# Second FFN's down projection and the per-layer embedding by blocks of 512 tokens, with bf16 copies of their weights in DRAM

## What is computed

```
h = x
h = h + 0.5 * rms(swiglu(rms(h), W_gate, W_up, W_down))        # FFN1, d_ff = 5632
h = h + rms(token_mixing(rms(h)))                              # 8 FoX attention heads, 8 HGRN2 heads, merge, W_out
h = h + 0.5 * rms(swiglu(rms(h), ...))                         # FFN2, same sizes
u = rms(h)
h = h + rms(sigmoid(u @ W_g) * (p @ W_p))                      # PLE; W_g is 2048 x 2048, p has 256 features
```

## Time and profile before

| | |
|---|---|
| median of 3 runs | 6165.52 us (6159.3 to 6673.99) |
| the profiled execution's own time | 6163.46 us |
| its span, slowest core (core 6) | 6161.9 us |
| spans of the 8 cores | 6130.3 to 6161.9 us |
| granted TensorE clock | 0.978 to 0.980 of full speed |
| PE busy | 5775.1 us, 94% of the span |
| DVE, ACT, POOL busy | 29%, 22%, 8% |
| DMA, mean over the span | 124 GB/s |

### The profile page before, as it was taken

One profiled execution on the slowest core, in us unless ns is written; L12 is line 12 of the kernel. 1 busy time (PEld: TensorE's weight loads), 2 busy tenths in 40 slices (PEclk: granted clock), 3 DMA queues, 4 the chain that ended last, 5 costly groups with the idle time before them and its releaser, 6 DMA issues.

```text
span 6161.9 us, 84644 instructions; the slowest of 8 cores (6130.3 to 6161.9 us)
## 1 busy us (share of the span) xinstructions
PE 5775.1 (94%) x30781; PEld 2799.5 (45%) x31334; DVE 1807.1 (29%) x3227; ACT 1326.5 (22%) x2391; POOL 469.4 (8%) x891
## 2 busy tenths in 40 slices
PE   5999999999999989999999999999999999999842
PEld 2444444444445556666444444444444444444321
DVE  2001022130203766555321333321110321110654
ACT  2000011111012444555312222211011111011321
POOL 0000000000000000000010010000000000000100
PEclk9999999999999999999999999999999999999976
DMA  6444488684756775343446879866475865475887
GB/s 144 76 76 78 83 160 166 115 157 76 144 105 125 151 159 106 67 80 70 93 79 127 171 150 194 170 118 117 74 155 105 163 127 108 84 148 101 180 185 171
DMA packets 317416, 763.89 MB, mean 124 GB/s; under 512 B 35280, under 2 KB 48720, under 8 KB 317008
## 3 DMA queue, kind: packets, MB, share of 16 engines
q0 software_dynamic: 127952, 422.67, 43.4%
q1 hardware_dynamic: 189056, 335.78, 20.1%
HBM read 1050.86 MB, written 130.06 MB: 192 GB/s over the span
## 4 chain that ended last, share of the span: by engine, by line
PE 87%; DMA 5%; DVE 4%; issue 2%; ACT 1%; SPq 1%; DVEq 0%; ACTq 0%
PE ps L459 87%; DMA out<-arena 3%; DVE arena L477 2%; DMA arena<-x 2%; DVE arena L487 1%; ACT arena L469 1%; SPq L510 1%; DMA arena<-h 1%; DMA arena<-ysp 0%; DVE arena L484 0%; DMA arena<-yfs 0%; DVE arena L497 0%; DVEq L249 0%; ACT L469 0%; DVE arena L503 0%
## 5 line engine op out<-in xcount | busy, mean ns | idle before, releaser
L459 PE MATMUL ps<-arena 128*128 128x512 bf16 (+2 forms) x30781 | 5775.1, 347 | 290.3 <-DVE arena L477 94.8
L459 PEld LDWEIGHTS ps<-arena 128*128 128x128 bf16 x31334 | 2799.5, 98 | 3265.4 <-issue 349.3
L477 DVE TENSOR_TENSOR arena<-arena 128x512 f32<-128x512 f32 (+7 forms) x1268 | 730.4, 592 | 1535.5 <-ACT arena L469 1388.4
L477 DVE TENSOR_TENSOR arena<-ps,arena 128x512 bf16<-128x512 f32 (+4 forms) x696 | 446.7, 642 | 2312.8 <-PE ps L459 2185.3
L469 ACT ACTIVATE arena<-ps 128x512 f32<-128x512 f32 (+1 forms) x864 | 515.4, 597 | 2542.0 <-PE ps L459 2457.0
L469 ACT ACTIVATE arena<-arena 128x512 f32<-128x512 f32 (+3 forms) x642 | 387.8, 616 | 753.0 <-DVE arena L477 676.5
L487 DVE SCALAR_TENSOR_TENSOR arena<-arena 128x512 f32<-128x512 f32 (+1 forms) x544 | 389.5, 743 | 329.4 <-DMA arena<-ysp 116.6
L495 ACT COPY arena<-ps 128x512 f32<-128x512 f32 x192 | 112.5, 586 | 1218.8 <-PE ps L459 1166.6
L469 ACT ACTIVATE arena<-ps,arena 128x128 bf16<-128x128 f32 (+2 forms) x576 | 257.6, 511 | 77.0 <-PE ps L459 74.8
L510 POOL DMA_DIRECT2D arena<-ffn_wg x176 | 93.2, 530 | 1729.3 <-PE ps L459 1686.2
L510 POOL DMA_DIRECT2D arena<-w_in x176 | 93.0, 529 | 1421.9 <-PE ps L459 1407.9
(11 more groups left out here) (18 smaller groups left out, 107.8 us busy)
## 6 DMA issues: line engine op xcount, KB each, us to landing
arena<-h SPq DMA_DIRECT2D x384, 256.0 KB, 7.1
arena<-ffn_wg POOLq DMA_DIRECT2D x176, 512.0 KB, 5.1
arena<-ffn_wu POOLq DMA_DIRECT2D x176, 512.0 KB, 6.4
arena<-w_in POOLq DMA_DIRECT2D x176, 512.0 KB, 6.6
arena<-ffn_wd POOLq DMA_DIRECT2D x128, 512.0 KB, 7.2
ysp<-arena SPq DMA_DIRECT2D x192, 256.0 KB, 7.3
arena<-ysp SPq DMA_DIRECT2D x192, 256.0 KB, 7.6
h<-arena SPq DMA_DIRECT2D x192, 256.0 KB, 6.9
```

The costliest lines, as they stand in the source:

```text
L459: ins = e.matmul(out.ap, l.ap, r.ap, start=st, stop=sp, skip_group_check=True)
L477: add(eng, lambda e: e.tensor_tensor(out=out.ap, in0=a.ap, in1=b.ap, op=op), C(a, b), out.cells, vdur(n, f) if eng == "dve" else 0.3 + n * ...
```

## The change

Three DRAM buffers take bf16 copies of the FFN2 down weights and of the two PLE weights; `copies` makes them with casting DMAs from DRAM to DRAM on POOL's queue, 80 in all (32.5 MB written), with 4 semaphores in turn. They are written into the program as background steps of `heads(1)`, `merge(0)` and `wout(0)`. `down` of FFN2's second half becomes two passes `down1`, one for each block, each of which loads all the weights, from the copies and without a cast. `ple` runs block by block, also from the copies. y of block 3 stays on chip (`y3`), and so does its residual; the last residual is made in place and stored with 6 semaphores in turn. At the start x of block 1 waits, tile by tile, for x of block 0, the weights of f = 1 to 3 wait for tile 8 of block 0, and the first 4 steps of `gateup` run for block 0, then for block 1.

```diff
+        xs = [av(M0 + t * 44 * K + 12 * K, (KC, TB), F32) for t in range(2)]
+        ub2 = av(M0, (KC, TB), BF16)
+        y3 = [av(M0 + (16 + 2 * i if i < 14 else 60 + 2 * i) * K, (TB,), F32) for i in range(KC)]
+        YR = Ring([av(M0 + 44 * K + i * 2 * K, (TB,), F32) for i in range(22)])
...
+        def wload(src, k0=0, nk=KC, more=(), cells=None, after=None):
             i, slot = wslots.next()
-            pairs = [(slot.s(slice(0, nk)), src[:, k0:k0 + nk, :])]
+            cc = (cells or []) + (after.cells if after is not None else [])
+            pairs = [(slot.s(slice(0, nk)), O(src[:, k0:k0 + nk, :], cc))]
...
-            dma("pool", "w%d" % i, pairs, o * 128 * 2 * 128, cast=True)
+            dma("pool", "w%d" % i, pairs, o * 128 * 2 * 128, cast=cells is None)
             return slot
+        cpy = Ring(list(range(4)))
+        def copies(pieces):
+            for dst, src, cell, n in pieces:
+                dma("pool", "cc%d" % cpy.next(), [(O(dst, [cell]), src)], n, cast=True)
+                yield
+        FQ = ((0, 16), (16, 16), (32, 12))
...
+        def post_ple(b, c0, n, ab, ys, hs=None):
+            gi = GI["ple_post"]
+            R = rstd_from(ab, n)
...
+            for dc in range(KC):
+                yt = ys[dc]
+                if hs is None:
+                    ht = load_tile("h3", dc, b).s(slice(c0, c0 + n))
+                else:
+                    ht = hs[dc].s(slice(c0, c0 + n))
+                stt(yt, yt, gsc.s(gi, slice(dc, dc + 1)), R, ALU.mult, ALU.mult)
+                tt(yt, ht, yt, ALU.add)
+                o = hd(out_d, "out", dc, b)
+                dma("sp", "po%d" % po_sem.next(), [(O(o.ap[:, c0:c0 + n], ...), yt)], 128 * n * 4)
+                yield
...
+            if first:                                  # in gateup
+                sl = []
+                for f in range(first):
+                    sl.append((wload(wg[f], after=xs[0].s(8) if f else None), wload(wu[f], after=xs[0].s(8) if f else None)))
+                for tb in range(2):
+                    for f in range(first):
+                        one(f, sl[f][0], sl[f][1], tb, 1 if tb == 0 and f < 2 else 4)
...
+        def down1(tb, b, bg, n, ys=None):
+            ab = None
+            for dc in range(KC):
+                step(bg, n)
+                sl = [wload(wdc_d[dc], f0, nf, cells=[("wdc", dc * 3 + q)]) for q, (f0, nf) in enumerate(FQ)]
+                py = bank_main.next()
+                for q, (f0, nf) in enumerate(FQ):
+                    mmd(py, sl[q], tb, nf, f0, q == 0, q == 2)
+                if ys is None:
+                    ab = y_out(py, tb, dc, b)
+                else:
+                    cp("act", ys[dc].s(), py.s(), boost=EV)
+                    ab = sq_acc(py.s(), accs[tb], dc, boost=EV)
+            return ab
...
+        def ple(u, c0, pt, p0, n, acc, bg=None, m=2):
+            ys, ab = [], None
+            cs = slice(0, n)
             for dc in range(KC):
-                step(bg, 4)
-                sg_ = wload(w_pg[dc])
-                sp = wload(w_pp[dc], 0, 2)
-                for tb in range(2):
...
+                step(bg, m)
+                sg_ = wload(pgc_d[dc], cells=[("pgc", dc), ("ppc", dc)])
+                sp = wload(ppc_d[dc], 0, 2, cells=[("pgc", dc), ("ppc", dc)])
+                y = YR.next().s(cs)
...
-                dma("sp", "sx%d" % dc, [(xs.s(dc, ts_), hcell("x", dc, b))], NBY)
+                dma("sp", "sx%d" % dc, [(xs[b].s(dc), O(x_.ap, xs[0].s(dc).cells if b else []))], NBY)
...
-        gateup("ffn1", u2[0])
+        gateup("ffn1", u2[0], first=4)
...
-        heads(1)
-        merge(0)
-        ab = wout(0)
+        wd2 = w["ffn2_wd"]
+        bg = copies([(wdc_d[dc][:, f0:f0 + nf], wd2[dc][:, f0:f0 + nf], ("wdc", dc * 3 + q), 128 * nf * 256)
+                     for dc in range(KC) for q, (f0, nf) in enumerate(FQ)])
+        heads(1, bg, 2)
+        flush(bg)
+        bg = copies([x for dc in range(KC) for x in ((pgc_d[dc], w_pg[dc], ("pgc", dc), 128 * KC * 256),
+                                                     (ppc_d[dc], w_pp[dc], ("ppc", dc), 128 * 512))])
+        merge(0, bg)
+        ab = wout(0, bg)
+        flush(bg)
...
-        ab = down("ffn2", 1, bg)
-        flush(bg)
-        bg = chain(*[g for b in (2, 3) for g in (post(b, ab[b - 2], "ffn2_post", "h2", "h3", res=res),
-                                                 pre(b, res, "ple_pre", "h3", u2[1], b - 2))])
-        ab = ple(0, bg)
-        flush(bg)
-        bg = chain(*[post(b, ab[b], "ple_post", "h3", "out", yple[b]) for b in (0, 1)])
-        ab = ple(1, bg)
-        flush(bg)
-        flush(chain(*[post(b, ab[b - 2], "ple_post", "h3", "out", yple[b]) for b in (2, 3)]))
+        ab2 = down1(0, 2, bg, 2)
+        flush(bg)
+        pt = [ple_in(0), ple_in(1)]
+        bg = chain(post(2, ab2, "ffn2_post", "h2", "h3", res), pre(2, res, "ple_pre", "h3", ub2, 0))
+        ab3 = down1(1, 3, bg, 2, y3)
+        flush(bg)
+        bg = post(3, ab3, "ffn2_post", "h2", None, res, y3)
+        ys, ab = ple(u2[0], 0, pt[0], 0, TB, accs[0], bg)
+        flush(bg)
+        pt.append(ple_in(2))
+        bg = chain(post_ple(0, 0, TB, ab, ys), pre(3, res, "ple_pre", None, u2[0], 0, y3))
+        ys, ab = ple(u2[0], TB, pt[1], 0, TB, accs[1], bg)
+        flush(bg)
+        pt.append(ple_in(3))
+        bg = post_ple(1, 0, TB, ab, ys)
+        ys, ab = ple(ub2, 0, pt[2], 0, TB, accs[0], bg)
+        flush(bg)
+        bg = post_ple(2, 0, TB, ab, ys)
+        ys, ab = ple(u2[0], 0, pt[3], 0, TB, accs[1], bg)
+        flush(bg)
+        flush(post_ple(3, 0, TB, ab, ys, y3))
```

More of the change, by code:

```diff
@@ L382, in build_program @@
         wfa = alloc((KC, 8), BF16)
-        pTb = [av(ST0 + (6 + i) * 2 * K, (2, TB), BF16) for i in range(2)] * 2
+        pTb = Ring([(i, av(ST0 + (6 + i) * 2 * K, (2, TB), BF16)) for i in range(2)])
         assert cur[0] <= TOT, cur[0] - TOT
@@ L606, in post @@
             gi = GI[gname]
             R = rstd_from(ab)
-            ab2 = None
             for dc in range(KC):
-                yt = load_tile("y", dc, b).s() if ysb is None else ysb.s(dc)
+                yt = load_tile("y", dc, b).s() if ys is None else ys[dc].s()
                 ht = load_tile(hin, dc, b)
                 stt(yt, yt, gsc.s(gi, slice(dc, dc + 1)), R.s(), ALU.mult, ALU.mult)
[L613 to L619, removed]
-                yield
@@ L622, in pre @@
-        def pre(b, res, gname, hname, u, tb):
+                if ys is None:
+                    i, ho = st_out.next()
+                    ho = ho.s()
+                else:
+                    ho = yt
+                tt(ho, ht.s(), yt, ALU.add)
+                if ys is None:
+                    store_tile("so%d" % i, ho, hout, dc, b)
+                ab2 = sq_acc(ho, acc2, dc, tmp=tmpp, ACB=ACP)
+                if ab2 is not None:
+                    res[b] = rstd_from(ab2)
+                yield
@@ L665, in y_out, with gateup, one @@
             return ab
-        def gateup(st, u, bg=None):
+        def gateup(st, u, bg=None, first=0):
             wg, wu = w[st + "_wg"], w[st + "_wu"]
-            for f in range(FC):
+            def one(f, sg_, su_, tb, grp):
+                p1 = bank_main.next()
+                p2 = bank_main.next()
+                if grp == 1:
+                    for k in range(KC):
+                        mmk(p1, sg_, u, tb, k, 1, k, k == 0, k == KC - 1)
+                        mmk(p2, su_, u, tb, k, 1, k, k == 0, k == KC - 1)
+                else:
+                    mmk(p1, sg_, u, tb, grp=grp)
+                    mmk(p2, su_, u, tb, grp=grp)
+                t = tmp.next()
+                sg = O(t.ap.bitcast(BF16)[:, 0:TB], t.s().cells)
+                act(sg, p1.s(), AF.Silu, boost=EV)
+                tt(aT[tb].s(f), p2.s(), sg, ALU.mult, boost=EV)
+            if first:
[5 more added lines that the diff above has]
+                        one(f, sl[f][0], sl[f][1], tb, 1 if tb == 0 and f < 2 else 4)
+            for f in range(first, FC):
                 sg_, su_ = wload(wg[f]), wload(wu[f])
                 for tb in range(2):
[L672 to L679, removed]
+                    one(f, sg_, su_, tb, KC)
                 step(bg, 1)
@@ L693, in down, with mmd @@
             return ab
+        def down1(tb, b, bg, n, ys=None):
[4 more added lines that the diff above has]
+                py = bank_main.next()
+                for q, (f0, nf) in enumerate(FQ):
+                    mmd(py, sl[q], tb, nf, f0, q == 0, q == 2)
+                if ys is None:
+                    ab = y_out(py, tb, dc, b)
+                else:
+                    cp("act", ys[dc].s(), py.s(), boost=EV)
+                    ab = sq_acc(py.s(), accs[tb], dc, boost=EV)
+            return ab
+        def mmd(py, slot, tb, nf, f0, first, last):
+            mmg([(py.s(), slot.s(k), aT[tb].s(f0 + k), first and k == 0, last and k == nf - 1) for k in range(nf)])
         def fox_gates():
```

(15 more changed lines are left out.)

81 lines of the change are left out of this document (41 added, 40 removed).

## The result

| | before | after |
|---|---|---|
| profiled execution | 6163.46 us | 6002.66 us |
| its span, slowest core | 6161.9 us (core 6) | 6001.1 us (core 3) |
| ratio of the compared runs | | 0.9744, 95% interval 0.9716 to 0.9772 |
| granted clock | 0.978 to 0.980 | 0.991 to 0.992 |

Forecast 6016, range 5945 to 6110.

A forecast was written before the change was run, and what follows sets the result against it. PE bounds the kernel, busy 98% from 103 to 5384 us, and loses time only at the start, a late hole and the end. 6163.5 - 169 (end) + 17 (gateup) + 5 (start) gives 6016, range 5945 to 6110.

The forecast's parts named there:

- end: From the last down on: the hole goes, 20 us of waits are charged, the tail shortens; 169 us less.
- waits in gateup: First gateup: copies put DMA 50 us behind PE, the slots cover 33; 17 us more.
- start: Until the steady run: four copies go ahead of block 0's x and outweigh its new order; 5 us more.
- heads: heads(1): no copies run there after all, so no change.
- Where the copies run: On POOL's queue from the first microseconds, through in the first gateup at about 480 us, not beside the heads.
- Rival A: Copies late or free for the start, block 0's x alone in front: 5952 us; chance 0.14, cheap copies included.
- A copy's price: DRAM to DRAM copy of 512 KB: 4.75 us of the DMA engines, the middle of 3.1 and 6.4.
- Rival B: Copies at the dear end, first gateup bound by DMA: 6126 us; chance 0.17.
- The look-ahead as cover: First gateup: weights asked for 41 us ahead land in 6.3, giving some 33 us of cover against 50.
- the new order of x: At the start: block 0's x first, block 0 beginning at 29 us and block 1 at 68; a gain of 42.
- The tail: Behind the last matmul: 36 us in place of 109.9.
- Rival C: Plain bf16 loads in down1 and ple bound by bytes written, 169 GB/s: 6173 us, slower than before; chance 0.07.

The follow-up runs named there:

- experiment 1: The kernel after, with the copies waiting for the last output of heads(0): 6009.6 us, ratio 0.9767.
- experiment 7: The kernel after, with each copy of the down and gate weights made twice, the second into buffers nobody reads: 6186.8 us.
- experiment 5: The kernel after, with copies waiting for the last tile of x of block 1 and one semaphore for four: 5961.2 us.
- experiment 6: The kernel after with one copy semaphore: 5965.0 us, ratio 0.9676; also with copies waiting for heads(0)'s last output: cores 0 to 3 end at 5940.9 to 5966.9.
- experiment 2: The kernel after, with the first copies waiting for the last tile of x of block 1, four semaphores kept: 5991.1 us.
- experiment 4: Two runs of the kernel before: with only the new last residual, 6122.1 us, ratio 0.9941; with only the new start, 6139.7 us, ratio 0.9949.
- experiment 8: The kernel after, copies behind block 1's x, one semaphore, block 1's squares and norm behind block 0's second step: 5937.2 us, repeated 5937.9, ratio 0.9637.
- experiment 3: The kernel after without copies; down1 and ple load the f32 weights with a cast, anew for each block: 6133.0 us, ratio 0.9958.

## Why the prediction was right

| term | predicted | measured | from |
|---|---|---|---|
| end | -169 | -192 | core 3, last down to the end |
| waits in gateup | +17 | +15 | gaps of PE from 160 to 720, core 3 (mean of the cores: 10) |
| start | +5 | +25 | core 3, matmuls done by 160 us |
| heads | none | -3 | core 3, PE from 1900 to 3100, 1143 to 1146 |
| sum | -147 | -155 | core 3: 6155.8 to 6001.1, -154.7 |

The time itself fell by 160.8 us, because the slowest core before was another (core 6, 6161.9). In the heads the mean of the cores gained 14 us, which no run explains.

**Where the copies run.** The planner's rule, read from w_fa, decided it: they began at 4.3 us and were through in the first gateup, at 597 us and not 480, because each DMA of POOL's list waits for its buffer or its semaphore, and these came as late as the full DMA engines let them. POOL's order was four copies, six weights and nine copies (forecast: about eight). Rival A falls; experiment 1 shows that to do what the listing says would have won nothing by itself.

**A copy's price.** 4.75 us was the middle of 3.1 and 6.4, taken because no row drew nearer to either: that it came so close is luck. By the estimates above it is 4.8 with four under way, 4.1 with one. The estimate from the Trainium skill ("DMA: Bandwidth & Descriptors", section "Latency and other measured facts") was 5.0; the 1.05 MB that a copy reads in 4.8 us are 218 GB/s, beside its 207 to 214, though that figure is for copies without a cast from other queues. Rival B, the dear end, falls.

**The look-ahead as cover.** The form of the sum (excess per step, less what eight slots hide) gave 17, and 15 came, by luck as well: carried on in experiment 7, the form missed by more than 100 us. What the wait hangs on is how many copies are under way ahead of a weight in the queue: experiment 5 moves as many bytes in 160 to 500 us without a wait. The cover isn't a stock of 33 us that is used up once; it is the 41 us of look-ahead against a landing time, 33 us here, 9 to 11 where copies come singly. That fits experiments 1 and 6 too, which the sum didn't foresee.

**The start: the step that was mis-sized.** I gave the new order of x 42 us and the copies 47 against it. Counted in matmuls done by 160 us (means of the cores, by their weight loads), it is 350 before, 227 after, 443 to 446 with the new order and no copy in its way (experiments 1, 2 and 4): the order brings 21 us, and the copies take 47. So the copies' part was right, and the whole error of the start lies in the order's. Two things were left out of the 42. The six weights that wait for tile 8 go out at 22 us, among the rest of block 0's x, and block 0 begins at 43 where I had 29; that the weights are the cause is argued, no run moves them. And block 1's 16 norm matmuls stand among block 0's steps in PE's order. Experiment 8 shows this one: with them moved back 14 us come. In the kernel itself the same fault shows: block 0 began at 55, earlier than the 65 to 75 forecast, but its f = 1 to 3 did not run while block 1's x came in, as the sum had it; they ran behind, from 115 to 137, and block 1 began at 144.5 where I had 114.

**The end.** 20 us of waits were charged, 1.8 came: no hand-over held PE, and at a DMA share of 0.95 PE waited for nothing. That the six PSUM banks and the eight slots covered it is likely, but no run varies them. The tail was 33.5, not 36. The plain loads ran at 311 GB/s where I took 298. Rival C falls, but experiment 3 shows what it feared, with loads that do run at the cast's rate: 172 us, as it had reckoned (165). As to what the gain is made of, the tail alone is 30 to 36 of the 192.

The total came within 14 us because the errors at the start (20) and at the end (23) had opposite signs; it was better than its parts, by luck.

## What to carry to other kernels

An operation without predecessors, in a list scheduler that never leaves an engine idle, is placed at time zero wherever it is written (here 80 copies from 4.3 us on); give it a dependency on the place where it is wanted. Side traffic in a shared queue cost, in these runs, by how many of its transfers were under way at once, ahead of the next one that matters: one cost PE nothing in gateup and 10 us in the heads, where four cost 10 to 22 and 45 to 55, for the same bytes. Weights that are read more than once because the work goes block by block are worth a bf16 copy, if the second read would otherwise bring the DMA engines over the time of the matmuls.

## What the runs showed of the hardware

A casting copy from DRAM to DRAM costs, by the two estimates, 4.1 to 4.8 us for 512 KB written, 1.3 to 1.5 times the casting load (3.1 to 3.4), not the sum of a load and a store (6.4). A plain bf16 load on POOL's queue writes at 311 GB/s, 1.8 times the cast's 169. DMA engines that are nearly full don't slow PE by themselves: at a share of 0.95 (ple after the change), and with q0 at 92.2% (gateup with one copy at a time), PE lost nothing; at 0.99 with four copies at a time beside the heads it lost 42 us of 300, against 9 without them.
